# Moving the gated recurrence of a Trainium2 kernel from three engines' shares to VectorE and ScalarE

## The reference

```python
f = lb_d + (1.0 - lb_d) * jax.nn.sigmoid(z)          # one forget gate for each direction
q = jax.nn.silu(q) * HG_HEAD_DIM ** -0.5
key, logf = 1.0 - f, jnp.log(f)
...
# S_t = diag(f_t) S_{t-1} + k_t v_t^T,  o_t = S_t^T q_t, from the context's final state
o_inter = einsum('bthk,bhkv->bthv', qb * exp(G), S)   # G: running sum of logf in a chunk
decay = exp(where(earlier_or_same, G[:, :, None] - G[:, None, :], -inf))
A = einsum('bthk,bshk,btshk->bhts', qb, kb, decay)
o_intra = einsum('bhts,bshv->bthv', A, vb)
S_new = exp(G_last)[..., None] * S + einsum('bshk,bshv->bhkv', kb * exp(G_last[:, None] - G), vb)
```

## Time and profile before

| | |
|---|---|
| median of 3 runs | 4615.64 us (4613.04 to 4617.64) |
| the profiled execution | 4615.48 us, its span 4613.7 us |
| TensorE busy | 3861.4 us, 84% |
| VectorE busy | 2639.6 us, 57% |
| ScalarE busy | 1952.4 us, 42% |
| GpSimd busy | 920.4 us, 20% |

### The profile page before, as it was taken

The page is one execution under the profiler, slowest core; times in us unless marked ns, Lnnn a source line. Parts: engine busy times, 40 slices in busy tenths (PEclk is TensorE's granted clock), DMA queues, the critical chain, the costliest instruction groups (busy, mean ns, idle before and its releaser), DMA issues. The chain is left out here.

```text
span 4613.7 us, 44330 instructions
## 1 busy us (share of the span) xinstructions
PE 3861.4 (84%) x17259; PEld 2898.2 (63%) x17259; DVE 2639.6 (57%) x2848; ACT 1952.4 (42%) x2610; POOL 920.4 (20%) x766
## 2 busy tenths in 40 slices
PE   6999797882556789999999998599888598997968
PEld 2888433342555427877777777478776276786736
DVE  6411355327775468888888887552166635514763
ACT  5411100014434317777767776533165314424631
POOL 0200243214542101101211111320022123201212
PEclk9999788986788899999999999799899798998979
DMA  7222215101003559999999997534320334333133
GB/s 266 96 103 85 91 48 186 34 26 60 22 23 136 194 197 346 373 370 364 370 370 363 374 370 288 189 116 127 116 76 8 138 113 142 119 107 127 46 106 122
DMA packets 392774, 785.34 MB, mean 170 GB/s; under 512 B 26006, under 2 KB 109089, under 8 KB 392242
## 3 DMA queue, kind: packets, MB, share of 16 engines
q1 hardware_dynamic: 376182, 730.87, 44.1%
q0 software_dynamic: 11456, 41.16, 2.8%
q10 hardware_dynamic: 4928, 10.49, 0.7%
HBM read 671.21 MB, written 111.25 MB: 170 GB/s over the span
## 5 line engine op out<-in xcount | busy, mean ns | idle before, releaser
L2342 DVE TENSOR_TENSOR moe_w_low<-moe_w_raw,moe_w_high 128x2048 fp32r<-128x2048 f32 x384 | 880.8, 2339 | 168.4 <-ACT moe_w_high L2295 167.6
L2295 ACT ACTIVATE moe_w_high<-moe_w_raw 128x2048 fp32r<-128x2048 f32 x384 | 715.0, 1913 | 304.4 <-DMA moe_w_raw<-in_exp_w 295.8
L172 PE MATMUL moe_bank<-moe_w_high,moe_xgT_high 128*128 128x512 f32 x1024 | 404.2, 395 | 17.1 <-DVE moe_w_low L2342 12.0
L174 PE MATMUL moe_bank<-moe_w_high,moe_xgT_low 128*128 128x512 f32 x1024 | 399.8, 390 | 0.0
L173 PE MATMUL moe_bank<-moe_w_low,moe_xgT_high 128*128 128x512 f32 x1024 | 399.3, 390 | 0.0
L2611 DVE TENSOR_REDUCE layer_att_nb<-layer_att_scores 128x1 f32<-128x1280 f32 (+1 forms) x144 | 197.1, 1369 | 143.0 <-PE layer_att_scores L2517 143.0
L172 PEld LDWEIGHTS moe_bank<-moe_w_high,moe_xgT_high 128*128 128x128 f32 x1024 | 192.7, 188 | 63.2 <-DVE moe_w_low L2342 15.8
L172 PE MATMUL layer_front_bank<-layer_front_w_high,layer_front_hT_high 128*128 128x512 f32 (+1 forms) x608 | 229.3, 377 | 0.0
L2604 POOL TENSOR_SCALAR layer_att_p<-layer_att_p,layer_att_rinv,layer_att_neg_lam 128x1280 f32<-128x1280 f32 (+1 forms) x72 | 95.2, 1323 | 669.7 <-DVE layer_att_rinv L2641 669.7
L174 PE MATMUL layer_front_bank<-layer_front_w_high,layer_front_hT_low 128*128 128x512 f32 (+1 forms) x608 | 223.2, 367 | 0.0
L173 PE MATMUL layer_front_bank<-layer_front_w_low,layer_front_hT_high 128*128 128x512 f32 (+1 forms) x608 | 223.1, 367 | 0.0
(11 more groups left out here) (447 smaller groups left out, 8944.1 us busy)
## 6 DMA issues: line engine op xcount, KB each, us to landing
moe_w_raw<-in_exp_w SPq DMA_DIRECT2D x192, 2048.0 KB, 10.4
mods_raw<-in_ada_w SPq DMA_DIRECT2D x12, 2048.0 KB, 8.7
h_raw<-in_w_mod SPq DMA_DIRECT2D x12, 2048.0 KB, 8.2
layer_front_raw<-in_w_in SPq DMA_DIRECT2D x48, 512.0 KB, 6.5
front_raw<-in_w_in SPq DMA_DIRECT2D x32, 512.0 KB, 6.3
proj_t<-front_out SPq DMA_DIRECT2D x48, 256.0 KB, 2.0
k_high<-layer_front_stageda SPq DMA_DIRECT2D x20, 512.0 KB, 3.3
k_low<-layer_front_stagedb SPq DMA_DIRECT2D x20, 512.0 KB, 4.7
```

The source lines that it names most:

```text
L172: nc.tensor.matmul(out, lhs[0], rhs[0], start=start, stop=False)
L174: return nc.tensor.matmul(out, lhs[1], rhs[0], start=False, stop=stop)
L2295: nc.scalar.activation(hi, x, ACT.Copy).then_inc(high, 1)
L2342: nc.vector.tensor_tensor(lo, x, hi.bitcast(F32), ALU.subtract).then_inc(low, 1)
```

## The change

VectorE now makes all products of the levels and of the carried keys and queries; GpSimd keeps two fills of constants at the stage's start. The scale and shift of the gates and of `q` move from VectorE to ScalarE (its Identity with scale and bias, and Copy with scale). The two subtractions of a level become one instruction of 512 elements, and so do the two products by keys: one access pattern takes the first half of each block from one direction's tensor and the second half from the other's (`halves`, `middles`). For that the two directions lie in one tensor, and the second direction's sums are kept negated. The preparation of the next head is cut in three: `keys` (with ScalarE's `forget_gates`) goes to the end of the first unit, `sums` around the second unit's first mask, `carried` after its third. Carrying the states is woven between level products.

```diff
-    WITH_TILE = [range(a, a + 1) if a < 3 else range(3, NSB) for a in range(NT // 2)]
+    WITH_TILE = [[], [0], [1, 2], [3, 4]]
-    ON_DVE = range(LEVELS, LEVELS + 4)
+        gates, X = st.sb("gates", [P, TL, P]), st.sb("x", [P, 2, TL, P])
+        def halves(tile, side, l, u):
+            half, d = P >> l + 1, TL * P
+            at = tile[:, side, u % 2 * UT, 0:P]
+            step = half + (d if side == 0 else -d)
+            return bass.AP(at.tensor, at.offset, [list(at.ap[0]), [2 * half, UT << l], [step, 2], [1, half]])
...
             @block.gpsimd
-                def prep(h):
-                        nc.gpsimd.tensor_tensor(kh[d][:, :, :], kh[d][:, :, :], k_[h % 2][d][:, :, :], ALU.mult)
-                        nc.gpsimd.tensor_tensor(qh[h % 2][d][:, :, :], qh[h % 2][d][:, :, :], q_[h % 2][:, :, :],
-                                                ALU.mult).then_inc(khd, 1)
-                def level(u, j):
...
             @block.scalar
+                def forget_gates(h):
+                    for d in range(2):
+                        core.act(act, nc.scalar.activation(z[d][:, :], z[d][:, :], ACT.Sigmoid))
+                        nc.scalar.activation(z[d][:, :], z[d][:, :], ACT.Identity, bias=core.lb[:, 0, c:c + 1],
+                                             scale=core.lb[:, 1, c:c + 1]).then_inc(fdone, 1)
+                    core.act(act, nc.scalar.activation(q_[h % 2][:, :, :], q_[h % 2][:, :, :], ACT.Silu))
+                    nc.scalar.activation(q_[h % 2][:, :, :], q_[h % 2][:, :, :], ACT.Copy, scale=float(P) ** -0.5).then_inc(qscaled, 1)
...
             @block.vector
-                    nc.vector.tensor_tensor(out[:, :, :, 0:half], ml, xl[:, :, :, 0:half], ALU.subtract)
-                    nc.vector.tensor_tensor(out[:, :, :, half:], xr[:, :, :, half:], mr, ALU.subtract).then_inc(dd, 1)
+                def exponents(u, j):
+                    a, b = (middles(side, l, u), halves(X, side, l, u))[::1 if side == 0 else -1]
+                    nc.vector.tensor_tensor(pieces(j, u), a, b, ALU.subtract).then_inc(dd, 1)
+                def level(u, j):
+                    dve.wait_ge(ed, u * NP + j + 1)
+                    if side:
+                        nc.vector.tensor_tensor(r, r, q_[b][:, t0:t0 + UT, :], ALU.mult).then_inc(rd, 1)
+                    else:
+                        nc.vector.tensor_tensor(r, r, halves(k_[b], 0, l, u), ALU.mult).then_inc(rd, 1)
```

More of the change, by code:

```diff
@@ L1749, in carry_state, with masks @@
                         dve.wait_ge(sdone, 2 * STEPS * h + s + 1)
-                prep(0)
+                def masks(h, t, b):
+                    n = h * NT + t
+                    m = NB * n + b
+                    dve.wait_ge(prod, m + 1)
+                    if n >= 2:
+                        dve.wait_ge(odone, n - 1)
+                    nc.vector.tensor_tensor(masked[m % 4][:, :, :], bank[m % 3][:, :].rearrange("p (i t) -> p i t", t=P),
+                                            mask[:, 4 * b:4 * b + 4, :], ALU.mult).then_inc(maskd, 1)
@@ L1752, in _ @@
+                keys(0)
+                sums(0, 0)
+                sums(0, 1)
+                for j in range(6):
+                    exponents(0, j)
+                carried(0)
+                for j in range(6, NP):
+                    exponents(0, j)
                 for k in range(NSB):
                     carry_state(0, k)
-                for j in range(NP):
-                    level(0, j)
+                    for j in range(3 * k, min(3 * k + 3, NP)):
+                        level(0, j)
@@ new lines, in _ @@
+                            masks(h, a, b)
+                            for i in range(4 * a + 2 * b, 4 * a + 2 * b + 2):
+                                for j in range(2 * i, min(2 * i + 2, NP)):
+                                    exponents(u + 1, j)
+                                if i >= 2:
+                                    level(u + 1, i - 2)
+                        if a == UT - 1 and h + 1 < H:
+                            keys(h + 1)
+                    more = h + 1 < H
+                    if more:
+                        sums(h + 1, 0)
@@ new lines, in _ @@
+                    masks(h, UT, 0)
+                    if more:
+                        sums(h + 1, 1)
+                    masks(h, UT, 1)
+                    if more:
+                        for j in range(6):
+                            exponents(u + 2, j)
+                    masks(h, UT + 1, 0)
+                    if more:
+                        carried(h + 1)
+                        exponents(u + 2, 6)
+                        exponents(u + 2, 7)
+                    masks(h, UT + 1, 1)
@@ new lines, in _ @@
+                    if more:
+                        for j in range(8, NP):
+                            exponents(u + 2, j)
+                        carry_state(h + 1, 0)
+                        level(u + 2, 0)
+                        level(u + 2, 1)
+                    masks(h, UT + 2, 0)
+                    if more:
+                        for j in range(2, 5):
+                            level(u + 2, j)
+                    masks(h, UT + 2, 1)
+                    if more:
+                        carry_state(h + 1, 1)
+                        level(u + 2, 5)
+                        level(u + 2, 6)
+                        carry_state(h + 1, 2)
@@ L1777, in stage_hgrn @@
+                    masks(h, UT + 3, 0)
+                    if more:
+                        for j in range(7, 10):
+                            level(u + 2, j)
+                    masks(h, UT + 3, 1)
+                    if more:
+                        carry_state(h + 1, 3)
+                        for j in range(10, NP):
+                            level(u + 2, j)
+                        carry_state(h + 1, 4)
         for j in range(2):
```

280 lines of the change are left out of this document (130 added, 150 removed).

## The result

The changed kernel takes 4542.72 us (median of 4 runs, 4535.96 to 4547.09) against 4614.99 before (4 runs): ratio 0.9843, 95% interval 0.9828 to 0.9857. It was forecast at 4535, in a range of 4522 to 4566.

A forecast was written before the change was run, and what follows sets the result against it. The bound was taken as VectorE's list, inflated by GpSimd and broken by a serial preparation per head. Savings of 67.5 (three heads), 10.5 (start) and 2.4 (last head) sum to 80.4 us: 4615.5 to 4535, range 4522 to 4566.

The forecast's parts named there:

- What bounds the kernel: Stage before the change: VectorE's list, inflated by GpSimd collisions, broken by one long serial preparation per 92.3 us head.
- Durations on VectorE: Start-to-start times from the old trace: 0.60 us for 512 elements or a mask, 1.41 for 1280 with two inputs.
- Rival A: Hopping pattern slow at the finest levels: 0.53 us more for three instructions a unit, 13 us, so 4548; chance 15%.
- Period of a head: First mask to next head's first mask: 69.8 us instead of 92.3, saving 67.5 us over three periods.
- level "by 0.3 us": Second unit's first bank at about 31.3 us, VectorE's scan and subtraction done at 31.6, so late copies cost nothing.
- TensorE needs 2.6 us from a mask's end to the result's copy: Duration used in each head for tile results, from a row where ScalarE idled 2.59 us.
- Rival B: Hand-overs between engines bind: three waits like 2.15 us lost per head, 20 us in all, so 4555; chance 17%.
- Before the first head: Stage's start to first mask: mask at 1090.7 against 1101.24, 10.5 us saved.
- Last head: First to fifth tile 24.8 us instead of 27.2, remaining four tiles keeping their pace: 2.4 us saved.
- ScalarE's four additional passes cost nothing on VectorE except the 2.1 us of the scan's wait: Per head, ScalarE's added gate and scale passes delay VectorE only by its 2.1 us wait for the logarithm.
- Slower (C): Merged pattern at contended pace in all levels: 1.74 us instead of 0.60 in 168 instructions, so 4718; chance 3%.
- no effect (D): The 0.94 us subtraction is the pattern's, not GpSimd's, so the gain shrinks: 64 us more, 4599; chance 2%.

The follow-up runs named there:

- pool_reads: Changed kernel plus 12 GpSimd products of 512 elements a unit on an unused tile, nothing waiting for them: stage 71.6 us longer, ratio 1.0001.
- pool_fills: Changed kernel plus 12 GpSimd constant fills of 512 elements a unit, which read nothing: stage 315.3 us against 315.2.
- before_nopool: Kernel before the change with GpSimd's level products cut to one channel a tile: stage 330.0 us against 387.2.
- one_piece: Changed kernel with the next head's preparation again in one piece before the second unit's first mask: program 4562 us, stage 333.8 against 315.2.
- halves_outer: Changed kernel with merged instructions going through all first halves, then all second halves: stage 6.6 us shorter.
- warm: Changed kernel with ten unused TensorE products ahead of tile 3's result in each head's first unit: stage 6.9 us shorter.
- copy2: Changed kernel with tile 2's result copy moved from behind the logarithm to behind the preparation's second Identity: stage 7.0 us shorter.

## Why the prediction was right, and what it mis-sized

- **What bounds the kernel:** a chain of preparation, and VectorE's list inflated by GpSimd. Right, and shown: `pool_reads`, `pool_fills`, `before_nopool` for the inflation, `one_piece` for the chain. The division is not in the prediction: 15.1 us less work on VectorE, 56.9 us less waiting.
- **Durations on VectorE:** right; 0.68 long and 0.60 from start to start for the merged subtraction in six levels of seven.
- **Rival A** was true in kind and mis-sized: 0.13 to 0.17 us, not 0.53, at blocks of two, nothing measurable at blocks of four. What costs is leaving the place of the last access with every element (`halves_outer`). I had weighed the rule of the Trainium skill (SBUF — State Buffer, "Door 1", the note on cachelines) as a rival: each access that crosses to a new 16-byte line pays a penalty, two hits in a line pay none. It is borne out in direction, 0.81 to 0.85 us against 0.68; the size is the runs'.
- **Period of a head: this is the term that was mis-sized.** 69.8 forecast, 73.4 measured, so three periods saved 56.6 and not 67.5. In the first head: the scan starts at 28.4 and not 27.3 (tile 1's result took longer, 4.26 us for its 16 products after 2.9 us without work, and its copy ended at 15.5 and not 15.0; ScalarE's chain took 12.7 and not 12.3, since an Identity with scale and bias takes 1.45 us and not 1.27); the mask after it comes 1.65 us late, which I had called level "by 0.3 us"; the rest of the head took 38.8 against 38.2. The step that failed is "TensorE needs 2.6 us from a mask's end to the result's copy", read off a row where TensorE had stood for 1.6 us and used where it had stood for 7.7 us, where it needs 4.6. `warm` and `copy2` show the mechanism. It is Rival B in kind, at 11 us and not 20. `warm` gives back 7.0 of these 11 us; the finest levels' pattern makes about 2.7 more, by my estimate (18 instructions by 0.15); ScalarE's longer passes are in the rest. I had slow values at hand: 2.2 against 1.15 us for a unit's first product, which I put down to the stage's start, and in the trace of before the result of a tile itself:

```profile
1174.46 3.78 PE L1633 MATMUL hgrn_bank<-hgrn_v,hgrn_masked 128*128 128x128 f32 x16 [5.02 <-ACT hgrn_ob L1571]
1178.04 1.06 PE L1638 MATMUL hgrn_bank<-hgrn_s,hgrn_qh 128*128 128x128 f32 x4
```

- **Before the first head:** 9.8 saved, 10.5 forecast.
- **Last head:** its first to fifth tile now takes 24.9 us, 24.8 forecast. But what it took before I read wrongly: the mask at 1405.29 is the second one of the fourth tile; the fifth tile's first is this one, so 5.6 us were saved there and not 2.4:

```profile
1408.64 0.69 DVE L1769 TENSOR_TENSOR hgrn_masked<-hgrn_bank,hgrn_mask 128x512 f32<-128x512 f32 x1 [2.66 <-PE hgrn_bank L1665]
```

- The sum: 56.6 + 9.8 + 5.6 = 72.0, 80.4 forecast. Two slips in opposite directions: the row that was misread hid 3 of the 11 us that the heads fell short, and that much of the closeness is luck.
- **"ScalarE's four additional passes cost nothing on VectorE except the 2.1 us of the scan's wait":** too low. The trace has three long ones (1.45, 1.45 and 1.06 us) and two of 0.21; `gates_dve` puts the three long ones back on VectorE, and the stage got 10.2 us shorter.
- **Slower (C) and no effect (D)** did not happen; the 0.94 us of the earlier trace rows was GpSimd's, as `pool_reads` shows.

## What to carry to other kernels

Before sharing elementwise work with GpSimd, look at like instructions of VectorE with and without GpSimd at work: a helper can cost more than it takes over, even where nobody waits for its products. When arithmetic is moved off a busy engine, ask whether that engine was waiting for the one that gets it. And take a duration of TensorE from a row with a like idle time in front of it, and look at the granted clock there: the stops of 5.0 and 7.7 us shown here were followed by slow values, one of 2.3 us by either.

## What the runs showed of the hardware that was not expected

- GpSimd's fills, 96 of 0.53 us, cost VectorE's `tensor_tensor` instructions nothing (`pool_fills`); its products of the same size cost 0.75 us each (`pool_reads`).
- A `tensor_tensor` of 512 elements whose access pattern changes between two tensors at every fp32 element takes 0.81 to 0.85 us and not 0.68; with the same elements in two runs of stride 2 it takes 0.68 to 0.70.
- A ScalarE Identity over 1280 elements with scale and bias read per partition takes 1.45 us; sigmoid, logarithm and exponential over as many, without them, take 1.25 to 1.27. No run has an Identity without them.
- After 7.7 us without work TensorE did 16 instructions in 3.78 us that it does in 1.95; its granted clock was 0.50 there. After a wait of 2.33 us the 14 instructions that open a unit took 1.83 us in one head and 3.36 in another of the same kernel, so a short wait may or may not bring it.
